# Expert tiles of 32 rows on four column groups of TensorE, in a two-layer diffusion trunk with a mixture of experts

## The reference

```python
def grouped_moe(h, router_w, router_b, w_gate, w_up, w_down):
    scores = sigmoid(h @ router_w)                       # 16 experts
    sel = (scores + router_b).reshape(n, 4, 4)           # 4 groups of 4
    best_group = argmax(sum of the two best of each group)
    expert_idx = the two best experts of the best group  # top-2
    gates = their scores, normalised to sum 1
    for e in range(16):
        a = silu(h @ w_gate[e]) * (h @ w_up[e])          # 1024 -> 512
        out = out + gates[:, e:e+1] * (a @ w_down[e])    # 512 -> 1024
```

## Time and profile before

| | us |
|---|---|
| device time, median of 3 runs (1117.69 to 1119.53) | 1119.21 |
| the profiled execution: its time | 1120.89 |
| the profiled execution: its span | 1119.3 |
| expert stage of layer 0 (first L1216 to the last product) | 364 to 647 |
| expert stage of layer 1 | 839 to 1087 |
| PE busy over the span | 969.8 (87%) |
| DVE, ACT, POOL busy | 308.2, 226.0, 102.5 |
| mean granted TensorE clock | 0.936 of full |

### The profile page before, as it was taken

The page is one execution under the profiler, slowest core; times in us unless marked ns, Lnnn a source line. Parts: engine busy times, 40 slices in busy tenths (PEclk is TensorE's granted clock), DMA queues, the critical chain, the costliest instruction groups (busy, mean ns, idle before and its releaser), DMA issues.

```text
span 1119.3 us, 16030 instructions
## 1 busy us (share of the span) xinstructions
PE 969.8 (87%) x5879; PEld 575.6 (51%) x5880; DVE 308.2 (28%) x695; ACT 226.0 (20%) x432; POOL 102.5 (9%) x174
## 2 busy tenths in 40 slices
PE   3799999999986999999999929999959988877980
PEld 2247434566446555555555516877445544544540
DVE  1104101864253111111111145357241111111113
ACT  2210102343020122122222223034021211111211
POOL 2000101004202200000000130000010000000002
PEclk9899999999995999999999969999959999999995
DMA  9977778549949698799999954646178999999973
GB/s 343 353 284 277 283 268 360 213 166 336 242 160 355 218 384 325 301 395 385 395 375 388 387 196 142 225 197 236 76 259 313 365 387 402 397 392 404 391 271 112
DMA packets 90564, 334.64 MB, mean 299 GB/s; under 512 B 9312, under 2 KB 23280, under 8 KB 74000
## 3 DMA queue, kind: packets, MB, share of 16 engines
q1 hardware_dynamic: 74112, 289.77, 67.9%
q0 software_dynamic: 10016, 33.89, 10.1%
q10 hardware_dynamic: 6400, 10.49, 2.7%
HBM read 307.84 MB, written 28.74 MB: 301 GB/s over the span
## 4 chain that ended last, share of the span: by engine, by line
PE 45%; DMA 18%; DVE 4%; issue 1%; ACT 1%; POOL 0%; ACTq 0%; SPq 0%; POOLq 0%; DVEq 0%
PE bank L1216 18%; DMA weight_ring<-in_w_up_dram 9%; PE bank L1234 9%; DMA weight_ring<-in_w_gate_dram 8%; PE bank L1014 3%; PE bank L1130 2%; PE bank L1017 2%; PE bank L1200 2%; PE bank L1261 2%; PE bank L1225 1%; PE bank L1092 1%; PE bank L1065 1%; DMA weight_ring<-y_by_expert,slot_numbers 1%; PE bank L1077 1%; PE bank L970 0%
## 5 line engine op out<-in xcount | busy, mean ns | idle before, releaser
L1216 PE MATMUL bank<-weight_ring,qk_tokens 128*64 128x256 f32 x2560 | 304.9, 391 | 32.6 <-DMA weight_ring<-in_w_up_dram 29.6
L1216 PEld LDWEIGHTS bank<-weight_ring,qk_tokens 128*64 128x64 f32 x2560 | 193.1, 141 | 139.8 <-issue 64.6
L1234 PE MATMUL bank<-weight_ring,qk_tokens 128*64 128x512 f32 x640 | 152.9, 598 | 0.0
L1622 DVE TENSOR_TENSOR qk_tokens<-qk_tokens,bank 64x256 f32<-64x256 f32 x80 | 33.8, 423 | 328.7 <-ACT qk_tokens L904 328.7
L1014 PE MATMUL bank<-weight_ring 128*128 128x256 f32 (+1 forms) x320 | 97.8, 464 | 4.9 <-ACT weight_ring L795 3.1
L1017 PE MATMUL bank<-weight_ring 128*128 128x512 f32 (+1 forms) x256 | 84.9, 489 | 0.0
L1130 PE MATMUL bank<-weight_ring 128*128 128x512 f32 x192 | 83.4, 594 | 1.4 <-ACT weight_ring L864 1.4
L1014 PEld LDWEIGHTS bank<-weight_ring 128*128 128x128 f32 x320 | 61.8, 196 | 40.3 <-issue 34.8
L904 ACT ACTIVATE qk_tokens<-bank 64x256 f32<-64x256 f32 x80 | 30.1, 376 | 206.2 <-PE bank L1216 205.9
L1234 PEld LDWEIGHTS bank<-weight_ring,qk_tokens 128*64 128x64 f32 x640 | 42.4, 136 | 54.2 <-issue 45.7
L904 ACT ACT_TABLE_LOAD x40 | 51.3, 1283 | 85.1 <-issue 74.9
(11 more groups left out here) (173 smaller groups left out, 731.4 us busy)
## 6 DMA issues: line engine op xcount, KB each, us to landing
weight_ring<-in_w_gate_dram SPq DMA_DIRECT2D x64, 1024.0 KB, 9.0
weight_ring<-in_w_up_dram SPq DMA_DIRECT2D x64, 1024.0 KB, 8.9
weight_ring<-in_w_down_dram SPq DMA_DIRECT2D x64, 1024.0 KB, 9.5
weight_ring<-in_w_mod_dram SPq DMA_DIRECT2D x24, 2048.0 KB, 8.1
weight_ring<-in_w_in_dram SPq DMA_DIRECT2D x12, 1024.0 KB, 10.0
qk_tokens<-h_by_expert POOLq DMA_DIRECT2D x40, 256.0 KB, 7.2
y_by_expert<-qk_tokens ACTq DMA_DIRECT2D x80, 128.0 KB, 7.0
weight_ring<-in_w_out_dram SPq DMA_DIRECT2D x4, 2048.0 KB, 11.7
```

The source lines that it names most:

```text
L1216: mm = pe.matmul(pb[hf][64 * r:64 * r + 64, 0:256], hTe[:, k, :], w[:, k, hf * 256:(hf + 1) * 256], start=(k == 0), stop=(k == KD - 1), ti ...
L1234: mm = pe.matmul(pb[4][64 * r:64 * r + 64, :], aTe[:, k, :], wdown(n)[:, k, r * 512:(r + 1) * 512], start=(k == 0), stop=(k == KF - 1), ti ...
L1622: V.tensor_tensor(ae[:, hf * 256:(hf + 1) * 256], sg[:, hf * 256:(hf + 1) * 256], pb[hf][SLOTS:P, 0:256], ALU.mult).then_inc(s_a[l], 1)
```

## The change

- `SLOTS` becomes 32. An expert has at least two tiles, and the buffers in memory hold 64 tiles of 32 rows. The product with the rows now occupies 32 columns of the array, and four products run side by side: in `gate_up` gate and up, each in two halves of 256 columns, all into one bank; in `down` four quarters of 256 output columns.
- PE's order changes: `gate_up(T)`, `turn_rows(T+1)`, `down(T-1)`, `turn_a(T)`. The down product is one tile late.
- The 32 rows of 1024 are held as 128 x 256: quarter q of the row on partitions 32q to 32q+31. A tile's rows are turned in two 128 x 128 transposes instead of eight, a product of silu and up in two instead of four. The columns of `h2` are stored in another order for this (`by_chunk`, `in_order`), and the router weights and expert weights are read in the matching order.
- Rows come through a ring of four tiles (`hring`). POOL loads a tile with four DMAs of 32 x 1 KB and waits until they have landed before it begins the next tile; ACT copies (`stage`) the tile from the ring to `hcur`, from which PE turns it.
- A tile's result is stored with four DMAs of 32 x 1 KB instead of two of 64 x 2 KB. As before, ACT copies the next result only when the stores of the last one have landed.
- The rows of the first four tiles are picked by PE as 128 rows: `picked` (128 x 128 per token tile) is the stationary operand and `h2` the moving one (512 columns), into two banks; ACT and DVE copy them into `hcur` and the ring.
- The unused rest of `ysort` is filled with zeros ahead, with 8 DMAs of POOL in layer 0, instead of the copies of L705 in the middle of layer 0.
- Waits for the table have a semaphore of their own (`s_tab`), earlier than `s_pos`.

```diff
-SLOTS = 64
+SLOTS = 32
-    NTILE = 2 * NALL * P // SLOTS + NE
+    NTILE = 2 * NALL * P // SLOTS + 2 * NE
+    AHEAD = P // SLOTS
+    Q = D // AHEAD
...
-        hrow = qkbuf[0:SLOTS, 0:1024]
-        hTe = qkbuf[:, 1024:1536].rearrange("p (k s) -> p k s", k=KD)
-        sg = qkbuf[SLOTS:P, 1536:2048]
-        ae = qkbuf[0:SLOTS, 2048:2560]
-        aTe = qkbuf[:, 2560:2816].rearrange("p (k s) -> p k s", k=KF)
-        ysb = qkbuf[:, 2816:3328]
+        hring = qkbuf[:, 0:AHEAD * Q]
+        hcur = qkbuf[:, 1024:1280]
+        hTe = qkbuf[:, 1280:1536]
+        sg = qkbuf[2 * SLOTS:P, 1536:1792]
+        ae = qkbuf[0:2 * SLOTS, 1536:1792]
+        aTe = qkbuf[:, 1792:1920]
+        ysb = qkbuf[:, 1920:2176]
...
-                        sp.wait_ge(s_gu[l], first * 2)
+                        sp.wait_ge(s_gu[l], first)
...
-                with pool.Fori(1, total) as T:
-                    pool.wait_ge(s_hTp[l], T + 1)
-                    pool.dma_start(hrow, hsort[bass.ds((T + 1) * SLOTS, SLOTS), :]).then_inc(s_hrow[l], 16)
+                with pool.Fori(0, rest) as n:
+                    pool.wait_ge(s_hc[l], n + 1)
+                    for q in range(AHEAD):
+                        pool.dma_start(hring[q * SLOTS:(q + 1) * SLOTS, bass.ds((n & (AHEAD - 1)) * Q, Q)],
+                                       hsort[bass.ds((n + AHEAD) * SLOTS, SLOTS), q * Q:(q + 1) * Q]).then_inc(s_hrow[l], 16)
+                    pool.wait_ge(s_hrow[l], n * 64 + 64)
...
+                def silu(T):
+                    act.wait_ge(s_gu[l], T + 1)
+                    nc.scalar.activation(sg, pb[0][0:2 * SLOTS, 0:Q], ACT.Silu).then_inc(s_si[l], 1)
+                def stage(T, src):
+                    act.wait_ge(s_hTp[l], T)
+                    nc.scalar.copy(hcur, src).then_inc(s_hc[l], 1)
+                def store_rows(T):
+                    act.wait_ge(s_d[l], T + 1)
+                    act.wait_ge(s_yd[l], T * 64 + 64)
+                    nc.scalar.copy(ysb, pb[4][:, 0:Q]).then_inc(s_y[l], 1)
+                    act.wait_ge(s_y[l], T + 2)
+                    for q in range(AHEAD):
+                        act.dma_start(ysort[slice(0, SLOTS) if isinstance(T, int) else bass.ds(T * SLOTS, SLOTS), q * Q:(q + 1) * Q],
+                                      ysb[q * SLOTS:(q + 1) * SLOTS, :]).then_inc(s_yd[l], 16)
...
+                with act.Fori(0, rest) as n:
+                    silu(n + 2)
+                    act.wait_ge(s_hrow[l], n * 64 + 64)
+                    stage(n + 4, hring[:, bass.ds((n & (AHEAD - 1)) * Q, Q)])
+                    store_rows(n + 1)
+                store_rows(rest + 1)
...
+                def gate_up(T, n, use, first):
+                    pe.wait_ge(s_hT[l], T + 1)
                     for k in range(KD):
+                        if first and k % HK == 0:
+                            arrived(n, 2 * (k // HK), use)
+                            arrived(n, 2 * (k // HK) + 1, use)
+                        for g in range(4):
+                            w, f = (wgate(n), wup(n))[g // 2], (g % 2) * Q
+                            mm = pe.matmul(pb[0][32 * g:32 * g + 32, 0:Q], hTe[:, (k % 2) * P + k // 2 * SLOTS:(k % 2) * P + (k // 2 + 1) * SLOTS],
+                                           w[:, k, f:f + Q], start=(k == 0), stop=(k == KD - 1), tile_position=(0, 32 * g))
+                    mm.then_inc(s_gu[l], 1)
...
+                def later_tiles(lo, hi, n, use):
+                    with pe.Fori(lo + 1, hi) as T:
+                        gate_up(T, n, use, False)
+                        turn_rows(T + 1)
+                        down(T - 1, n, use, True)
+                        turn_a(T)
```

More of the change, by code:

```diff
@@ L680, in _ @@
                     pool.wait_ge(s_zeros, 1)
-                    for n in range(NTILE):
-                        pool.dma_start(hsort[n * SLOTS:(n + 1) * SLOTS, :], zeros).then_inc(s_hz, 16)
+                    for n in range(NZ):
+                        pool.dma_start(hsort[n * P:(n + 1) * P, :], zeros).then_inc(s_hz, 16)
+                    for n in range(NZ - NZ // 2, NZ):
+                        pool.dma_start(ysort[n * P:(n + 1) * P, :], zeros).then_inc(s_yz, 16)
                 for t in range(NT[l]):
@@ L901, in _ @@
[L901 to L904, removed]
+                act.sem_inc(s_yd[l], 64)
+                act.wait_ge(s_yz, 16 * (NZ // 2))
+                def silu(T):
+                    act.wait_ge(s_gu[l], T + 1)
+                    nc.scalar.activation(sg, pb[0][0:2 * SLOTS, 0:Q], ACT.Silu).then_inc(s_si[l], 1)
@@ new lines, in _ @@
+                act.wait_ge(s_first.sem, s_first.at(l, 1))
+                for T in range(AHEAD):
+                    dst = hcur if T == 0 else hring[:, T * Q:(T + 1) * Q]
+                    for q in range(2):
+                        ins = nc.scalar.copy(dst[q * SLOTS:(q + 1) * SLOTS, :], pb[6][T * SLOTS:(T + 1) * SLOTS, q * Q:(q + 1) * Q])
+                    if T == 0:
+                        ins.then_inc(s_hc[l], 1)
+                ins.then_inc(s_firstA.sem, 1)
+                act.wait_ge(s_firstA.sem, s_firstA.at(l, 1))
@@ L1251, in expert @@
-                def expert(e, use, n):
-                    lo = pe.value_load(tab[l][0:1, bass.ds(e, 1)], min_val=0, max_val=NTILE)
-                    hi = pe.value_load(tab[l][0:1, bass.ds(e + 1, 1)], min_val=0, max_val=NTILE)
-                    with pe.Fori(lo, hi) as T:
-                        tile(T, n, use)
-                pe.wait_ge(s_pick.sem, s_pick.at(l, 1))
-                for k in range(KD):
-                    for t in range(NT[l]):
-                        mm = pe.matmul(pb[5][:, k * SLOTS:(k + 1) * SLOTS], model_rows(h2[:, t, :], k), picked[:, t, :],
-                                       start=(t == 0), stop=(t == NT[l] - 1))
@@ new lines, in down @@
+                def down(T, n, use, first):
+                    pe.wait_ge(s_aT[l], T + 1)
+                    pe.wait_ge(s_y[l], T + 1)
+                    for k in range(KF):
+                        if first and k % 2 == 0:
+                            arrived(n, 4 + k // 2, use)
+                        for g in range(4):
+                            mm = pe.matmul(pb[4][32 * g:32 * g + 32, 0:Q], aTe[:, (k % 2) * 2 * SLOTS + k // 2 * SLOTS:(k % 2) * 2 * SLOTS + (k // 2 + 1) * SLOTS],
+                                           wdown(n)[:, k, g * Q:(g + 1) * Q], start=(k == 0), stop=(k == KF - 1), tile_position=(0, 32 * g))
+                    mm.then_inc(s_d[l], 1)
@@ new lines, in expert @@
+                def expert(e, n, use):
+                    lo = pe.value_load(tab[l][0:1, bass.ds(e, 1)], min_val=2, max_val=NTILE - 2)
+                    hi = pe.value_load(tab[l][0:1, bass.ds(e + 1, 1)], min_val=2, max_val=NTILE - 2)
+                    gate_up(lo, n, use, True)
+                    turn_rows(lo + 1)
+                    down(lo - 1, n - 1, use, False)
+                    turn_a(lo)
+                    later_tiles(lo, hi, n, use)
+                pe.wait_ge(s_tab.sem, s_tab.at(l, 1))
@@ L1271, in _ @@
+                down(total - 1, NE - 1 + l, (NE - 1) // RING + 1, False)
         @block.vector
```

213 lines of the change are left out of this document (104 added, 109 removed).

## The result

The changed kernel takes 1181.45 us (median of 4 runs, 1177.41 to 1183.24) against 1118.8 before in the same runs: ratio 1.056, 95% interval 1.053 to 1.059. It is slower by 62.7 us. The prediction had it slower, by 101 us, at 1220.

A forecast was written before the change was run, and what follows sets the result against it. PE was taken to bound layer 0's expert stage and weight loads layer 1's. Span 1119.3 + 99 for tiles paced by store and row-load waits + 2.6 for tails made 1221, median 1220; range 1104 to 1272, the forecast's own 1190 to 1250.

The forecast's parts named there:

- PE's tile: PE in the expert stages: one tile of 32 rows takes 6.6 us, with gate_up 3.84 and down 1.92.
- ACT's loop: Result stores on ACT: copy, four issues and the last landing, 7.0 us after its issue, take 9.55 us per tile.
- The rival of a turn per DMA: Stores behind the weights: landings spaced 1.25 to 1.85 us, loop 11.4 or 13.2, time 1264 or 1300; chance 0.17.
- POOL's loop: Row loads on POOL: four issues and a landing of 7.2 us take 9.4 to 10.3 us per tile.
- The two loops together: ACT's stores and POOL's row loads feed one another at a little over the longer: 9.8 us per tile while weights load.
- The sum: Both expert stages: 46.3 tiles at 9.8 us and 26.7 at 6.6 give 630 us against 531, so +99.
- The weights would wait for slots: Weight loads in the expert stages: 2.5 tiles need 24 us, an expert's load 17.5; layer 1 falls below 390 GB/s.
- First rows: Picking the first tiles' rows on PE ahead of each stage: taken as 0, with -7 and +2 us as bounds.
- The strided h2: DVE operations writing `h2` with a stride: 0 to +2.5 us per layer, taken as 0.
- The faster rival: Expert stages: small DMAs land sooner and the loops stay under PE, 1108 us; chance 0.20.
- the case called in between: Expert stages: a loop of 8.2 us, each DMA landing in 5.6, time 1161; chance 0.12.
- The rival of a whole 1 MiB share for each turn: Stores behind the weights: loop of 16.4 us, time 1344; chance 0.06, shared with a PE bound by records.

The follow-up runs named there:

- the two-buffer kernel: Changed kernel with a second result buffer, copies waiting for stores of two tiles before, and row loads for the load two before: 1100.6 us, ratio 0.984.
- its halves: Changed kernel with only the second result buffer: 1176.81 us; with only row loads that wait for the load two before: 1171.83 us.
- the quarter of the weights: Changed kernel whose looped weight loads fetch only a quarter of each part, waits untouched, output differs: 1077.8 us, ratio 0.964.
- the last experiment: Changed kernel with one 32 KB DMA in place of four in ACT's store loop and POOL's row load, output differs: 1076.51 us, ratio 0.961.

## Why the prediction was right in sign and too high

The mechanism was right: ACT's copy waits for `y_by_expert`, POOL for its own load, PE's work as a whole did not grow (265.3 + 218.5 = 483.8 us busy in both windows, against 500.4 in rows 2), and the tiles come at the pace of these two loops while weights load. Shown by the two-buffer kernel and its halves, and from the other side by the quarter of the weights. Step by step:

- **Tiles, 73.** Right.
- **PE's tile, 6.6.** 6.20, and 0.8 us at the change of an expert: 6.6 in the mean of layer 0 in the last experiment. gate_up 3.66 against 3.84, down 1.93 against 1.92.
- **ACT's loop, 9.55.** This is the term that was mis-sized, with POOL's: 8.6 measured. The three issues cost 1.47, not 1.9, and the fourth DMA lands 6.6 after its issue, not 7.0. The spacing of landings is 1.0, not 1.25 to 1.85; each DMA has half the packets and a quarter of the bytes of those pairs; which of the two makes the shorter turn is not shown. The rival of a turn per DMA was right that the landings queue up, and wrong to add them to a first landing of 7.0: the first is in after 5.0. A first landing of 5.0 and three steps of 1.0 is how 8.0 comes about.
- **POOL's loop, 9.4 to 10.3.** 9.17 in the first tiles of layer 0, with landings of 5.6 to 6.8 against 7.2 assumed. 5.04 where no weights load, against 5.4 assumed.
- **The two loops together, 9.8.** 9.17 in layer 0 and 8.5 in layer 1 ((1049.33 - 1032.29)/2). Each is the pace of one loop alone; the addition for two loops that feed one another doesn't show.
- **The sum, 630.** By its own form, with these values: 227/9.17 = 24.8 tiles while loading and 15.2 x 6.6 make 327 for layer 0; 227/8.5 = 26.7 tiles and 6.3 x 6.6 make 269 for layer 1. 596, against 589 measured and 630 forecast. So 34 of the 41 us too much are the size of the loop.
- **The weights would wait for slots and layer 1 fall below 390 GB/s.** Right for layer 0: an expert's loads begin 24 us after the last one's in the first part of the stage, which is the number forecast, and the rate falls from 354 to 311 GB/s. Wrong for layer 1: with 2.1 tiles to an expert, 2.1 x 8.6 = 18 us of tiles stand against 16.9 of loads, and the rate stays near 400. There the weights load on, and the last tiles are worked off behind them at PE's own pace, from 1112 to 1142.
- **First rows, 0 (-7 to +2).** -5.1 in layer 0, for all that lies ahead of the stage. The 16 products (348.08 in PE's timeline) took 8.96 us, between the 7.13 and the 14 of the forecast.
- **The strided h2, 0 (0 to +2.5 a layer).** Mis-sized: 0.7 us more for each operation, two a tile, so 5.6 us of DVE's time in layer 0 and 2.8 in layer 1. In layer 1 all four stand in the chain that ended last (838.48 to 849.8), so the 2.8 are paid there; all between the stages grew by 1.7, and what gained the difference was not looked into.
- **Tails, +2.6 in both layers.** The stretch behind layer 1 grew by 1.6, against 1.3 for one layer.
- **The clock.** 0.95 and 0.96 in the two stages, as allowed for. With the gaps gone it is 1.00 in layer 0.

1181 lies between the case called in between (1161, a loop of 8.2) and the forecast's own range, which began at 1190: inside the wide range, outside the one that the forecast gave itself. The faster rival is what the change becomes when the two waits are taken away: it was put at 1108 (layer 0 at 272, layer 1 at 246), though the range was then begun at 1104 in its name, and the two-buffer kernel has 1100.6, with 265 and 245. The rival of a whole 1 MiB share for each turn (1344) is out: the landings are 1.0 apart.

## What to carry to other kernels

When tiles get smaller, list what is waited for once per tile, above all each landing of a DMA behind a stream of big loads; it shrinks far less than the tile (5.2 us for 32 KB here, 7.0 for 128 KB), and it binds as soon as the compute of a tile falls below it. Give each such loop a second buffer, in both directions at once: one alone gave 5 or 10 of the 81 us. Merge DMAs only after a look at the outermost dimension of both sides. On ACT's queue the number of packets showed that fewer engines took part; on POOL's it did not tell.

## What the runs showed of the hardware

- One store with an outermost dimension of 4 left 132 packets and took mostly 12 to 16 us behind the weights in layer 0; four stores of the same bytes are all in after 8.0.
- A landing follows the load on the engines more than the size: 32 KB took 1.5 us with nothing beside it, 2.8 with a quarter of the weights, 5.2 with all; 128 KB took 7.0 with all.
- fp32 operations of DVE on 128x1024 in SBUF took 1.9 to 2.1 us with a stride, whether in what is read or in what is written, and 1.2 to 1.3 without.
